# A sparse expert layer on one core: an expert's tokens as rows of a DRAM copy by an indirect DMA and transposes, in place of products with the slots' table

## The reference, cut to what matters

```python
def moe_swiglu(h, w_router, w1, w3, w2):
    logits = (h @ w_router).astype(jnp.float32)
    top_v, top_i = lax.top_k(logits, TOP_K)          # 2 of 8 experts a token
    top_w = jax.nn.softmax(top_v, axis=-1)
    combine = jnp.sum(jax.nn.one_hot(top_i, N_EXPERTS) * top_w[..., None], axis=-2)
    out = jnp.zeros_like(h)
    for e in range(N_EXPERTS):
        out = out + combine[..., e:e + 1] * swiglu(h, w1[e], w3[e], w2[e])   # 1024 -> 3584 -> 1024
    return out
```

## Time and profile before

| | |
|---|---|
| median of 3 runs | 1739.85 us (1739.45 to 1740.13) |
| the profiled execution's own time | 1740.86 us |
| its span | 1739.1 us |
| PE busy | 1659.2 us (95%) |
| DVE busy | 1417.8 us (82%) |
| ACT busy | 1147.6 us (66%) |
| POOL busy | 69.1 us (4%) |
| mean granted clock of PE | 0.973 |

### The profile page before, as it was taken

One profiled execution on the slowest core, in us unless ns is written; L12 is line 12 of the kernel. 1 busy time (PEld: TensorE's weight loads), 2 busy tenths in 40 slices (PEclk: granted clock), 3 DMA queues, 4 the chain that ended last, 5 costly groups with the idle time before them and its releaser, 6 DMA issues.

```text
span 1739.1 us, 24399 instructions
## 1 busy us (share of the span) xinstructions
PE 1659.2 (95%) x8014; PEld 1372.7 (79%) x8014; DVE 1417.8 (82%) x1696; ACT 1147.6 (66%) x1401; POOL 69.1 (4%) x194
## 2 busy tenths in 40 slices
PE   6999979999979997799999999999999999999997
PEld 5977758878779776688888888888888888888885
DVE  7867867787685466588989898899889889899888
ACT  4656344434345664477887877877877878878775
POOL 0020010000001101400000000000000000000000
PEclk9999989999989999699999999999999999999998
DMA  9954647767556343189989899899899899899894
GB/s 386 395 210 178 253 166 275 276 266 271 217 233 249 124 151 140 49 316 365 358 327 383 326 360 376 318 371 373 321 371 375 324 367 368 325 372 363 324 374 179
DMA packets 72832, 512.07 MB, mean 294 GB/s; under 512 B 8963, under 2 KB 10188, under 8 KB 10828
## 3 DMA queue, kind: packets, MB, share of 16 engines
q1 hardware_dynamic: 72496, 511.26, 77.8%
q10 hardware_dynamic: 284, 0.13, 0.0%
HBM read 510.30 MB, written 1.06 MB: 294 GB/s over the span
## 4 chain that ended last, share of the span: by engine, by line
PE 87%; DVE 6%; issue 3%; ACT 2%; POOL 1%; DMA 0%; DVEq 0%; ACTq 0%; POOLq 0%
PE ps L1235 27%; PE ps L1237 26%; PE ps L1236 26%; DVE wlo L295 2%; PE ps L1582 2%; PE ps L1467 2%; DVE wide L1035 1%; PE ps L1330 1%; ACT whi L288 1%; DVE x L787 1%; ACT L288 1%; DVE wide L702 0%; PE ps L1259 0%; PE ps L1350 0%; DMA qk<-in_rel_bias 0%
## 5 line engine op out<-in xcount | busy, mean ns | idle before, releaser
L295 DVE TENSOR_TENSOR wlo<-raw,whi 128x1024 fp32r<-128x1024 f32 x872 | 1019.0, 1221 | 159.0 <-ACT whi L288 158.8
L288 ACT ACTIVATE whi<-raw 128x1024 fp32r<-128x1024 f32 x872 | 872.9, 1053 | 261.7 <-PE ps L1237 257.3
L1235 PE MATMUL ps<-whi,hhi 128*128 128x512 f32 x1376 | 546.3, 397 | 8.0 <-DVE hlo L1019 4.1
L1236 PE MATMUL ps<-whi,hlo 128*128 128x512 f32 x1376 | 539.2, 392 | 0.0
L1237 PE MATMUL ps<-wlo,hhi 128*128 128x512 f32 x1376 | 538.5, 391 | 0.0
L1235 PEld LDWEIGHTS ps<-whi,hhi 128*128 128x128 f32 x1376 | 260.3, 189 | 66.2 <-issue 8.6
L1237 PEld LDWEIGHTS ps<-wlo,hhi 128*128 128x128 f32 x1376 | 260.3, 189 | 55.6
L1236 PEld LDWEIGHTS ps<-whi,hlo 128*128 128x128 f32 x1376 | 260.6, 189 | 53.4 <-issue 1.0
L1235 PE MATMUL ps<-whi,ohi 128*128 128x512 f32 x624 | 249.6, 400 | 3.1 <-DVE gate L768 2.0
L1237 PE MATMUL ps<-wlo,ohi 128*128 128x512 f32 x624 | 243.9, 391 | 0.0
L1236 PE MATMUL ps<-whi,olo 128*128 128x512 f32 x624 | 243.2, 390 | 0.0
(11 more groups left out here) (214 smaller groups left out, 1073.5 us busy)
## 6 DMA issues: line engine op xcount, KB each, us to landing
raw<-in_w_moe SPq DMA_DIRECT2D x336, 1024.0 KB, 7.1
raw<-in_w_pre_moe SPq DMA_DIRECT2D x100, 1024.0 KB, 4.9
raw<-in_w_mod_units SPq DMA_DIRECT2D x48, 1024.0 KB, 5.3
x<-in_x SPq DMA_DIRECT2D x1, 1024.0 KB, 5.2
bias<-dist_scratch SPq DMA_DIRECT2D x1, 1024.0 KB, 7.8
out<-x SPq DMA_DIRECT2D x2, 512.0 KB, 2.7
condb<-in_c SPq DMA_DIRECT2D x1, 512.0 KB, 6.7
qk<-in_bucket_onehot ACTq DMA_DIRECT2D x1, 49.4 KB
```

The costliest lines, as they stand in the source:

```text
L288: nc.scalar.activation(whi[:, s % SPLIT, part], raw[:, slot(s), part], ACT.Copy).then_inc(hi_done, 1)
L295: nc.vector.tensor_tensor(wlo[:, s % SPLIT, part], raw[:, slot(s), part], whi[:, s % SPLIT, part].bitcast(F32), ALU.subtract).then_inc(lo_ ...
L1235: nc.tensor.matmul(out, a_hi, b_hi, start=first, stop=False, **kw)
L1236: nc.tensor.matmul(out, a_lo, b_hi, start=False, stop=False, **kw)
```

## The change

The normed tokens `xn` are also written to a DRAM tensor `xn_rows` (256 rows of 4 KB), once, by two transfers that ACT issues after `norm(3)`. POOL makes a table `tokid` of the tokens' numbers at the start. For each expert PE multiplies `gat` by `tokid` (two products of one column into bank 7, `slot_tokens`), which gives the token's number for each slot; DVE copies that column to `idx`; POOL issues an indirect DMA that fetches the 128 rows into `rows` (a free part of `qk`); and PE transposes the rows into banks 2 and 3 (`rows_T`, eight transposes of 128 x 128). This, and ACT's `expert_tokens`, stand after the first two blocks; on PE, ACT and DVE these two are taken out of the loop, which has two passes left. The first expert's tokens still come by `gather`. The code:

```diff
-          rel_bias, w_router, moe_units, onehot_d, dist_scratch, out_d):
+          rel_bias, w_router, moe_units, onehot_d, dist_scratch, xn_rows, out_d):
...
+        rows = qk[:, 2048:3072]
...
         cur = sb("cur", [P, 2, C])
         ctl = sb("ctl", [P, 8])
         ctli = sb("ctli", [P, 8], I32)
+        tokid = sb("tokid", [P, C])
+        idx = sb("idx", [P, 1], mybir.dt.uint32)
+        spare = sb("spare", [P, 1])
         rowsM = qk[0:DEPTH * MODS, 2048:2048 + P]
         rowsB = qk[0:64, 2176:2176 + P]
...
+        tokid_set = sem("tokid_set")
+        rows_out = sem("rows_out")
+        rows_in = sem("rows_in")
+        idx_ps = sem("idx_ps")
+        idx_sb = sem("idx_sb")
...
             out_squares(2)
             norm(3)
+            for c in range(C):
+                act.wait_ge(xn_done, C * 3 + c + 1)
+                act.dma_start(xn_rows[c * P:(c + 1) * P, :], xn[:, c, :]).then_inc(rows_out, 16)
             act.wait_ge(rexp_in, 1)
             nc.scalar.activation(rt[:, 9, :, 0], rt[:, 8, :, 0], ACT.Exp).then_inc(rexp, 1)
...
                         act.wait_ge(cnt_sb, 1)
                         act.wait_ge(ylo_done, i * 2 + 2)
                         clear_sums()
-                expert_tokens(i + 1, 0)
-                expert_tokens(i + 1, 1)
                 ffn_ghi(1, i * FBLK, 0, hidden_half(0))
-                with act.Fori(0, (FBLK - 1) // 2) as tt:
+                def two_blocks(tt):
                     for q in range(2):
                         block_steps(1, MOE0 + 4 + 6 * q, i * FBLK + tt * 2, i * FBLK + tt * 2 + (q + 1),
                                     hidden_half(q + 1))
+                two_blocks(0)
+                expert_tokens(i + 1, 0)
+                expert_tokens(i + 1, 1)
+                with act.Fori(0, (FBLK - 3) // 2) as tt:
+                    two_blocks(tt + 1)
                 act.wait_ge(unit_used, i * FFN_UNITS + (MOE0 + FFN_UNITS - 4))
                 expert_hi(i + 1)
                 for j in range(2):
...
                         combine(i, j - 1)
                     if j == 3:
                         ffn_g(1, i * FBLK, i * FFN_UNITS + (MOE0 + 4))
+                        dve.wait_ge(idx_ps, i + 1)
+                        nc.vector.tensor_copy(idx[:], bank[7][:, S:S + 1]).then_inc(idx_sb, 1)
                         ffn_glo(1, i * FBLK, 0, hidden_half(0))
-                with dve.Fori(0, (FBLK - 1) // 2) as tt:
+                def two_blocks(tt):
                     for q in range(2):
                         s0 = MOE0 + 4 + 6 * q
                         t = i * FBLK + tt * 2 + q
...
                             split_lo(dve, s0 + j + LEAD, i * FBLK + tt * 2)
                             if j == 3:
                                 ffn_g(1, t + 1, i * FFN_UNITS + tt * 12 + (s0 + 4))
+                two_blocks(0)
+                with dve.Fori(0, (FBLK - 3) // 2) as tt:
+                    two_blocks(tt + 1)
                 expert_lo(i + 1)
                 for j in range(2):
                     split_lo(dve, MOE0 + FFN_UNITS + j, i * FBLK)
...
             nc.gpsimd.memset(relx, NEG).then_inc(relx_set, 1)
+            nc.gpsimd.iota(tokid[:], pattern=[[P, C]], base=0, channel_multiplier=1,
+                           allow_small_or_imprecise_dtypes=True).then_inc(tokid_set, 1)
             nc.gpsimd.iota(iota[:], pattern=[[1, P]], base=0, channel_multiplier=0,
                            allow_small_or_imprecise_dtypes=True).then_inc(const, 1)
             for tile in (ident, upper, lower):
...
                 nc.gpsimd.tensor_copy(cur[:, 1, :], wI[:, :, bass.ds(i, 1)].rearrange("p c o -> p (c o)"))\
                     .then_inc(wcur_done, 1)
+            pool.wait_ge(ctl_done, 1)
+            pool.wait_ge(rows_out, 16 * C)
             def expert(i):
-                pool.wait_ge(ctl_done, 1)
                 weights(i)
+                pool.wait_ge(idx_sb, i + 1)
+                pool.wait_ge(gath_done, i * 2 + 2)
+                nc.gpsimd.tensor_tensor(spare[:], tokid[:, 0:1], tokid[:, 1:2], ALU.add)
+                nc.gpsimd.indirect_dma_start(rows, None, xn_rows, bass.IndirectOffsetOnAxis(ap=idx[:, 0:1], axis=0))\
+                    .then_inc(rows_in, 16)
             with pool.Fori(0, E) as i:
                 expert(i)
...
                     ins = nc.tensor.matmul(bank[4][:, c * E:(c + 1) * E], h32[:, k, c * P:(c + 1) * P], wr[:, k, :],
                                            start=k == 0, stop=k == KC - 1)
             ins.then_inc(lg_done, 1)
+            pe.wait_ge(tokid_set, 1)
             gate_rows(3)
             pe.wait_ge(mem_done, 1)
             mem = rt[:, 7, :, :]
...
                         ins = nc.tensor.matmul(bank[2 + half][:, k * P:(k + 1) * P], xn[:, c, kk * P:(kk + 1) * P],
                                                gat[:, c, :], start=c == 0, stop=c == C - 1)
                 ins.then_inc(gath_done, 1)
+            def rows_T(item):
+                pe.wait_ge(rows_in, item * 16)
+                for half in range(2):
+                    for k in range(4):
+                        kk = 4 * half + k
+                        ins = nc.tensor.transpose(bank[2 + half][:, k * P:(k + 1) * P], rows[:, kk * P:(kk + 1) * P],
+                                                  ident[:])
+                    ins.then_inc(gath_done, 1)
+            def slot_tokens(i):
+                pe.wait_ge(gat_done, i * 2 + 4)
+                pe.wait_ge(gatT_sb, i + 2)
+                for c in range(C):
+                    ins = nc.tensor.matmul(bank[7][:, S:S + 1], gat[:, c, :], tokid[:, c:c + 1], start=c == 0,
+                                           stop=c == C - 1)
+                ins.then_inc(idx_ps, 1)
             def slots_T(item):
                 for c in range(C):
...
                         combine(i, j - 1)
                     if j == 2:
                         slots_T(i)
-                pe.wait_ge(comb_add, i * 4 + 5)
-                gather(i + 1, 0)
-                gather(i + 1, 1)
+                slot_tokens(i)
                 hidden_T(1, i * FBLK, 0)
-                with pe.Fori(0, (FBLK - 1) // 2) as tt:
+                def two_blocks(tt):
                     for q in range(2):
                         s0 = MOE0 + 4 + 6 * q
                         t = i * FBLK + tt * 2 + q
...
                                 expert_down(s0 + j, i * FBLK + tt * 2, j - 4, q)
                             if j == 4:
                                 hidden_T(1, t + 1, 0)
+                two_blocks(0)
+                pe.wait_ge(comb_add, i * 4 + 5)
+                rows_T(i + 1)
+                with pe.Fori(0, (FBLK - 3) // 2) as tt:
+                    two_blocks(tt + 1)
                 pe.wait_ge(gl_done, i * FBLK + (base_of[1] + FBLK))
                 for j in range(2):
                     expert_down(MOE0 + FFN_UNITS - 2 + j, i * FBLK, j, FBLK - 1, last=j == 1)
...
-    build(nc, *args, scratch, out)
+    rows = nc.dram_tensor("xn_rows", (S, D), F32, kind="Internal").ap()
+    build(nc, *args, scratch, rows, out)
```

## The result

Before and after on one chip, median of four runs each: 1739.65 us (1739.02 to 1740.13) and 1758.03 us (1757.61 to 1760.42). The ratio is 1.0109 with a 95% interval of 1.0091 to 1.0126. The change makes the kernel 18.4 us slower; the forecast was 15.3 us slower.

A forecast was written before the change was run, and what follows sets the result against it. PE was taken to bound the middle of an expert, DVE's 13.35 us in a row its start. Eight x (-0.4 + 0.9 + 0.1) = +4.8, plus 10.5 for the clock, gave +15.3: 1755.2 us, range 1743 to 1766.

The forecast's parts named there:

- The start, -0.4 an expert: At each expert's start, removing the gather's 3.84 us on PE gains only 0.4 us, because hidden_T then waits for ffn_g.
- `slot_tokens`, nothing: Its two small products on PE, at most 0.7 us, end two microseconds before ffn_g and so cost nothing.
- `rows_T`, +0.9: Eight transposes on PE after an expert's second block, all on the path, cost 0.9 us an expert.
- The third block, +0.1: ACT's moved token work uses up the 1.1 us slack before ffn_g, so PE stalls about 0.1 us an expert.
- The clock, 1.5 at seven of eight, +10.5: PE's hole at an expert's start lowers its clock, costing 1.5 us at 7 of 8 experts, 10.5 in all.
- the two waits on which the prediction built: PE waits of 2.77 and 2.19 us in the trace before, cited as followed by a granted clock of 0.50.
- The transfer and POOL, nothing: Fetched rows have 34 us to land (skill estimate 3.2), and POOL is nearly idle, so both cost nothing.
- The sum: Eight experts at -0.4 + 0.9 + 0.1 give +4.8 us; with +10.5 for the clock, +15.3 us.
- the third rival: POOL's new instructions hold DVE up, or rows come late or loops don't stay loaded: 1767 us; chance 0.10.
- The clock holds: Rival: PE's clock does not fall at the experts' starts, leaving only +4.8 us, 1744.7 us; chance 0.17.
- The saving is real: Rival: ffn_g comes 2.3 us earlier or more, so 2.1 us less an expert, 1723.0 us; chance 0.06.

The follow-up runs named there:

- e5: The changed kernel with ffn_g moved ahead of expert_slots, gatT copy and split on DVE, and slot_tokens behind the next block's first unit on PE: 1729.57 us.
- e1: The changed kernel with nine idle products of 512 columns on PE between slot_tokens and hidden_T: 1746.33 us, 1.0037 of before.
- e1b: The changed kernel with four idle products of 512 columns on PE between slot_tokens and hidden_T: 1753.61 us, 1.0084 of before.
- e2: The kernel before with only 4 of the 16 products of each gather in the loop, nothing added or moved: 1745.11 us, 1.0023 of before.
- e3: The changed kernel without the indirect DMA; a small POOL addition signals instead and the rows hold a constant: 1760.01 us, 1.0112 of before.
- e9: e5 with the second combination moved into PE's wait for ffn_g, and slot_tokens and the idx copy one unit later: 1720.15 us, 0.9887 of before.
- e6: The kernel before with ffn_g ahead of expert_slots on DVE and hidden_T ahead of the gather on PE: 1744.78 us, 1.0031 of before.
- e8: e5 with DVE's unexecuted program for items beyond the eight left out: 1727.12 us, 0.993 of before.

## Why the prediction was right, point by point

- *The start, -0.4 an expert.* Right. Measured -0.48 + 0.06 = -0.42. `ffn_g` took the gather's place, 2.26 us of wait at seven of the starts and 1.75 at the first. The first `hidden_T` was 1.1 us earlier still; the rows put that ahead of the loop, where the clock's level differed between the two executions, and that it fell on this side is luck.
- *`slot_tokens`, nothing.* Right in the hole: L1635 ends at 994.64, 2.2 us before `ffn_g` does. e5 shows its price without that cover, 0.36 us, a little under the 0.4 to 0.7 given.
- *`rows_T`, +0.9.* Right: 0.79 us to the next unit's start and 0.13 in that unit, 0.92.
- *The third block, +0.1.* The stall that was forecast did not come: `ffn_g` ended at 1046.80, in time, and no wait stands there. That the block is 0.13 longer is the unit behind `rows_T`.
- *The clock, 1.5 at seven of eight, +10.5.* The mechanism was right and the size near: it fell at all eight, at 1.46 us by the difference to e1, 11.7 (1.6 by the periods within e1b and within e2). e1 shows it as a cause: nothing but busy products in the hole gives it back. e2 shows that it needs nothing of the change but the hole, and also that a fall is not certain there. Of the two waits on which the prediction built, the one of 2.19 us was followed by 0.54 and not quite 0.50.
- *The transfer and POOL, nothing.* Right. POOL's instruction took 0.98 us, and DVE's next one was waiting for ACT in any case; e3, without the transfer, is no faster. The rival had the price on the wrong engine: where the two met, in e5 and e9, POOL waited and DVE did not. The Trainium skill (SBUF — State Buffer, Who interferes with whom) says that a VectorE instruction with two SBUF inputs and a GpSimd instruction that reads SBUF contend, and that issue order decides who blocks; the 6.70 us of POOL's addition in e9, which started 0.25 us after DVE's six splits had begun and lasted through all six, agree with it. The estimate of 3.2 us from the Trainium skill (DMA: Bandwidth & Descriptors, section Anatomy of one DMA) is under the 5.8 us measured from issue to landing, beside the stream of weights; neither is near the 34 us that were free.
- *The sum.* What was missing is the exit of the loop, +2.1 us once. The prediction had it only as a remark in the third rival ("loops that no longer stay loaded"), priced together with POOL and not on its own. With it and the 1.1 us from ahead of the loop, the forecast's 15.3 becomes 16.3, against 16.6 between the two traces; the medians differ by 18.4, of which 1.6 are the two profiled executions' places among the others.
- *The rivals.* "The clock holds" came out as e1, 5.2 us slower for 4.8 foretold, of which 2.1 are the exit of the loop, which that price did not have. "The saving is real" asked for `ffn_g` 2.3 us earlier, with a win from 0.6 on; e5 made it that much earlier and won. It was a rival of another kernel, not of this one.

## What to carry to other kernels

Before removing work from the engine that is busiest, look at what the next instruction on it waits for: here 3.84 us of PE's work stood in the shadow of 13.3 us of DVE's, and taking it out was worth 0.4 us. A hole on TensorE has a second price, its clock; in the kernel after each of the eight cost another 1.5 us, more than the saving. The same removal became a gain of 19 us once the operation that it waited for was taken ahead on DVE and other work was put into the hole, so the order on the releasing engine and the removal should be planned together. And when two traces are compared, compare periods of the loop: the way to its first unit alone differed by up to 6 us between traces of this case.

## What the runs showed of the hardware

- The clock fell at seven of seven starts with 3.67 to 3.70 us between the last unit and `hidden_T` and 0.6 us of four small records in it, and at the first start with 2.09 us, 1.75 of them a wait (the kernel after); at five of eight with waits of 0.49 and 2.04 us around 1.2 us of products (e2); at three of the seven later starts with a last wait of 1.2 us, and not at the first, where that wait was 0.69 (e1b); at the one start with a wait of 1.96 us (e9); at none of sixteen with one wait of 0.96 us (e5, e6). Equal holes did not give equal answers.
- One fall cost 1.46 us by the difference between the kernel after and e1, and 1.60 and 1.61 us by the periods with and without a fall within the traces of e1b and e2.
- An indirect transfer of 128 rows of 4 KB kept POOL busy for 0.98 us and landed 5.8 us after its issue (4.6 to 7.7), no later than the weights' units of 1 MB beside it (6.8).
- A small addition on POOL that took 0.19 us with DVE idle took 1.08 us (e5) and 6.70 us (e9) when DVE's splits, with two inputs from SBUF, ran; the splits did not get longer.
- DVE stood still for 2.8 us at a branch past a body that isn't executed, and for none of it with the body taken out (e5, e8). In the kernel before, which has such a body too, its combination started 0.09 us after PE's product.
